# Half-made output tiles: starting an attention block's output projection on the heads that are already finished

## What is computed

```
o_fox = fox_attention(fq, fk, fv, log_f)                 # 8 heads of 64, a forget gate
o_nsa = nsa_attention(nq, compress(kc), compress(vc),     # 8 heads of 64; three branches:
                      ks, vs, kw, vw, gates)              #   compressed, selected, window
y = concatenate([o_fox, o_nsa], axis=-1) @ w_out          # [512,1024] @ [1024,1024]
x = x + rms_norm(y, g[1])
mem_n = rms_norm(mem, mem_norm_g)                         # 256 memory rows
x = x + rms_norm(memory_cross_attention(rms_norm(x, g[2]), mem_n, ...), g[3])
```

## Time and profile before

| | |
|---|---|
| time, median of 3 runs | 2358.0 (2357.14 to 2361.31) |
| profiled execution: its time | 2356.57 |
| profiled execution: its span | 2354.6 |
| PE busy | 2195.7 (93%) |
| DVE, ACT, POOL busy | 53%, 47%, 31% |
| granted TensorE clock, mean | 0.969 |

### The profile page before, as it was taken

The page is one execution under the profiler, slowest core; times in us unless marked ns, Lnnn a source line. Parts: engine busy times, 40 slices in busy tenths (PEclk is TensorE's granted clock), DMA queues, the critical chain, the costliest instruction groups (busy, mean ns, idle before and its releaser), DMA issues.

```text
span 2354.6 us, 29885 instructions
## 1 busy us (share of the span) xinstructions
PE 2195.7 (93%) x10776; PEld 1776.7 (75%) x10776; DVE 1239.3 (53%) x2212; ACT 1118.4 (47%) x1964; POOL 726.9 (31%) x479
## 2 busy tenths in 40 slices
PE   8989999989999999988979999999988888999997
PEld 6656677767888787766867888887867767888886
DVE  6776575558999634555455232224467455332223
ACT  6455554467888535545343332224666344322222
POOL 4361233410000221511234333225833424333233
PEclk9999999999999999998989999999999989999999
DMA  4402233218999530220212232331311221332331
GB/s 165 151 24 68 72 104 107 72 72 306 394 387 394 190 102 25 72 81 1 90 63 67 96 100 96 99 99 63 99 54 37 72 72 48 98 105 91 99 99 54
DMA packets 74529, 264.10 MB, mean 112 GB/s; under 512 B 8272, under 2 KB 8400, under 8 KB 74000
## 3 DMA queue, kind: packets, MB, share of 16 engines
q1 hardware_dynamic: 66816, 238.76, 29.3%
q0 software_dynamic: 2816, 11.82, 1.4%
q10 hardware_dynamic: 4752, 11.61, 1.3%
HBM read 247.98 MB, written 14.18 MB: 111 GB/s over the span
## 4 chain that ended last, share of the span: by engine, by line
PE 80%; DVE 7%; ACT 6%; issue 3%; POOL 2%; DMA 2%; POOLq 0%; DVEq 0%; SPq 0%; ACTq 0%
PE ps L512 17%; PE ps L514 17%; PE ps L513 17%; PE ps L1144 3%; PE ps L574 2%; PE ps L1159 2%; PE ps L2855 2%; PE ps L2857 2%; PE ps L2856 2%; PE ps L1178 2%; PE ps L550 2%; PE ps L551 2%; PE ps L556 2%; PE ps L2882 1%; PE ps L2883 1%
## 5 line engine op out<-in xcount | busy, mean ns | idle before, releaser
L454 ACT ACTIVATE wh<-raw 128x1024 fp32r<-128x1024 f32 x308 | 322.3, 1054 | 443.4 <-PE ps L514 413.2
L459 DVE TENSOR_TENSOR wl<-raw,wh 128x1024 fp32r<-128x1024 f32 x176 | 238.8, 1363 | 512.7 <-ACT wh L454 507.5
L459 POOL TENSOR_TENSOR wl<-raw,wh 128x1024 fp32r<-128x1024 f32 x132 | 318.2, 2411 | 489.1 <-ACT wh L454 473.2
L512 PE MATMUL ps<-hh,wh 128*128 128x512 f32 (+1 forms) x1192 | 468.0, 393 | 0.3 <-DVE wl L459 0.3
L514 PE MATMUL ps<-hh,wl 128*128 128x512 f32 (+1 forms) x1192 | 464.5, 390 | 0.0
L513 PE MATMUL ps<-hl,wh 128*128 128x512 f32 (+1 forms) x1192 | 464.4, 390 | 0.0
L512 PE MATMUL ps<-act,wh 128*128 128x512 f32 (+1 forms) x688 | 270.5, 393 | 13.8 <-ACT act L1419 9.9
L513 PE MATMUL ps<-act,wh 128*128 128x512 f32 (+1 forms) x688 | 268.5, 390 | 0.0
L514 PE MATMUL ps<-act,wl 128*128 128x512 f32 (+1 forms) x688 | 268.3, 390 | 0.0
L512 PEld LDWEIGHTS ps<-hh,wh 128*128 128x128 f32 (+1 forms) x1192 | 223.7, 188 | 48.9 <-issue 2.1
L514 PEld LDWEIGHTS ps<-hh,wl 128*128 128x128 f32 (+1 forms) x1192 | 223.5, 188 | 47.6 <-issue 0.6
(11 more groups left out here) (468 smaller groups left out, 3887.1 us busy)
## 6 DMA issues: line engine op xcount, KB each, us to landing
raw<-d_w SPq DMA_DIRECT2D x277, 512.0 KB, 3.7
raw_x<-d_moe SPq DMA_DIRECT2D x84, 512.0 KB, 6.4
raw<-d_moe SPq DMA_DIRECT2D x84, 512.0 KB, 6.6
d_xs<-Sb POOLq DMA_DIRECT2D x7, 514.0 KB, 8.8
Xb<-d_xs ACTq DMA_DIRECT2D x6, 514.0 KB, 6.0
area<-d_mem POOLq DMA_DIRECT2D x3, 1024.0 KB, 6.5
d_ys<-rows ACTq DMA_DIRECT2D x6, 512.0 KB, 6.3
xT<-d_x SPq DMA_DIRECT2D x8, 256.0 KB, 6.7
```

What stands on the lines that cost most here:

```text
L454: me.e.activation(hi, raw, ACT.Copy).then_inc(*me.done("wh", m))
L459: me.e.tensor_tensor(lo, raw, hi.bitcast(F32), ALU.subtract).then_inc(*me.done("wl", m))
L512: me.e.matmul(bank[0:m, 0:n], wh[:, c], hi, start=k == 0, stop=False)
```

## The change

The attention functions of ACT and DVE get a hook `last`, called in their closing step. There, and in POOL's program behind its attention, `fox_out` now splits the four "of" chunks, with a narrower wait list. PE, after its last attention step, begins the output tiles n = 0, 1, 2 on chunks 0 to 3 only (`begun_pe`, 12 matmuls each), one before and two behind what is left of the compressed branch; `sandwich_pe` later adds chunks 4 to 7 to them. The blocks of the weights change order accordingly: tile A (the first) holds the first halves of n = 0 and n = 1, tile B the first half of n = 2 and the second of n = 0, tile C the second halves of n = 1 and n = 2; D is n = 3, E is n = 4, as before.

```diff
-def linear(K, me, key, name, layer, columns, src, m=128, n=T, row0=0, after=None, pool="ps", amid=None):
-    bank = K.banks[me.take(pool, *key)]
-    for k, (hi, lo, ready) in enumerate(src):
+def linear(K, me, key, name, layer, columns, src, m=128, n=T, row0=0, after=None, pool="ps", amid=None, ks=None):
+    k0, k1 = ks or (0, len(src))
+    bank = K.bank(*key) if k0 else K.banks[me.take(pool, *key)]
+    for k in range(k0, k1):
+        hi, lo, ready = src[k]
...
-    if after is not None:
+    if after is not None and k1 == len(src):
         me.give(pool, key, *after)
...
+        if last and step > len(pairs):
+            last(K, me)
         if step > 1:
             scales_act(K, me, a, p - 1, pairs[p - 1][0])
...
+def begun_pe(K, me, v, name, n, src, k1):
+
+    linear(K, me, ("sw", v, n), name, 0, cols(128 * n, 128 * n + 128), src, ks=(0, k1))
+    K.plan.tile["begun", v, n] = (len(K.plan.blocks) - 1) // 8 if K.plan.dry else K.plan.tile["begun", v, n]
...
-        linear(K, me, ("sw", v, n), name, layer, cols(128 * n, 128 * n + 128), src, after=[("y", v, n)])
+        linear(K, me, ("sw", v, n), name, layer, cols(128 * n, 128 * n + 128), src, after=[("y", v, n)],
+               ks=(begun[1] if n < begun[0] else 0, len(src)))
...
     attention_pe(K, me, "nsa", K.i_branch, ticks=2)
     me.alias("hfree", "n4")
+    outs = K.parts(0, 4, 4, "of") + K.parts(8, 12, 4, "on")
+    for n in range(3):
+        begun_pe(K, me, "x4", "ev_w_out_2", n, outs, 4)
+        me.tick(2)
     me.flush()
     me.alias("end", "pe", "nsa")
-    sandwich_pe(K, me, "x4", "ev_w_out_2", 0, K.parts(0, 4, 4, "of") + K.parts(8, 12, 4, "on"), "mem1")
+    sandwich_pe(K, me, "x4", "ev_w_out_2", 0, outs, "mem1", (3, 4))
...
+def fox_out(K, me):
+
+    ahead(K, me, ("begun", "x4", 0))
+    war = [("S", "nsa", 7, h, g) for h in range(2) for g in range(3) if h == 0 or g != 1] + [("S", "nsa", 7, 1, 1)]
+    war += [("cmp", "s", half) for half in range(2)] + [("xin", s, half) for s in range(2) for half in range(2)]
+    parts_of(K, me, "of", 4, 0, lambda c: K.area[:, 20 + c, :], [("whole", "of", c) for c in range(4)], war)
...
 def even_out(K, me):
     war = [("end", "pe", "nsa"), ("end", "dve", "nsa")]
-    parts_of(K, me, "of", 4, 0, lambda c: K.area[:, 20 + c, :], [("whole", "of", c) for c in range(4)], war)
     parts_of(K, me, "on", 4, 8, lambda c: K.O[:, c, :], [("cmp", "add", c) for c in range(4)], war)
...
     attention_pool(K, me, "nsa", K.i_branch, ticks=2)
+    fox_out(K, me)
     me.flush()
```

More of the change, by code:

```diff
@@ L1319, in attention_pe, with attention_act @@
     me.alias("end", "pe", a)
-def attention_act(K, me, a, items, first=(), pt_first=(), ticks=0):
+def attention_act(K, me, a, items, first=(), pt_first=(), ticks=0, last=None):
     pairs = pairs_of(items)
@@ L1336, in attention_act, with attention_dve @@
     me.alias("end", "act", a)
-def attention_dve(K, me, a, items, first=(), pt_first=(), ticks=0):
+def attention_dve(K, me, a, items, first=(), pt_first=(), ticks=0, last=None):
     pairs = pairs_of(items)
@@ L2220, in residual_pool, with sandwich_pe @@
         values_pool(K, me, ("mv", side), K.mem_values(side))
-def sandwich_pe(K, me, v, name, layer, src, side=None):
+def begun_pe(K, me, v, name, n, src, k1):
+    linear(K, me, ("sw", v, n), name, 0, cols(128 * n, 128 * n + 128), src, ks=(0, k1))
+    K.plan.tile["begun", v, n] = (len(K.plan.blocks) - 1) // 8 if K.plan.dry else K.plan.tile["begun", v, n]
+def sandwich_pe(K, me, v, name, layer, src, side=None, begun=(0, 0)):
     for n in range(DC):
@@ L3574, in even_act @@
     me.beside = compressed_side(K, me)
-    attention_act(K, me, "nsa", K.i_branch, [("end", "pe", "fox")], [("pv", "fox", 3)], ticks=2)
+    attention_act(K, me, "nsa", K.i_branch, [("end", "pe", "fox")], [("pv", "fox", 3)], ticks=2, last=fox_out)
     me.flush()
@@ L3599, in even_dve @@
     K.o_last = [("out", "nsa", c) for c in range(4)]
-    attention_dve(K, me, "nsa", K.i_branch, [("end", "pe", "fox")], [("pv", "fox", 3)], ticks=2)
+    attention_dve(K, me, "nsa", K.i_branch, [("end", "pe", "fox")], [("pv", "fox", 3)], ticks=2, last=fox_out)
     me.flush()
```

## The result

| | before | after |
|---|---|---|
| time, median of 20 runs each | 2357.21 (2351.22 to 2362.66) | 2363.07 (2355.29 to 2373.28) |
| ratio, with 95% interval | | 1.0024 [1.0014, 1.0034] |
| profiled execution: time, span | 2356.57, 2354.6 | 2360.35, 2358.5 |
| granted clock, mean | 0.969 | 0.966 |

A forecast was written before the change was run, and what follows sets the result against it. The memory's chain sets the start of n = 3, with PE only 1.08 behind; spreading 2.9 later plus 2.0 for the clock makes +4.9, and 2358.0 + 4.9 = 2362.9, range 2357.8 to 2367.0.

The forecast's parts named there:

- Begun halves on PE: At the end of attention, PE starts the begun halves at 1109.0, with a gap of some 1.5 instead of 3.64.
- "On" halves 3.0 later: ACT's "on" halves wait for tile A's end on PE and start at 1115.6 instead of 1112.58.
- Load 2.0 later: The memory load, queued behind POOL's "on" low halves, is issued at 1120.1 instead of 1118.11.
- The load's landing, 7.2: The memory load lands 7.2 after issue, 0.7 of it for a weight load issued within 1 of it.
- The Trainium skill's round robin: DMA engines alternate between queues, so the weight load costs the memory load 2.0 instead of 0.7; sum 1.3 higher.
- Landing to root, 8.4: From the memory's landing to PE's spreading takes 8.4, against 8.1, with POOL's low half of E beside DVE's sums.
- The 6.2: Lower end for landing to PE's spreading, if POOL and DVE don't meet.
- Spread 2.9 later: PE's spreading matmuls ahead of n = 3 come at 1135.7 instead of 1132.77.
- 7 to 8 was forecast: Sign in the profile after: PE waits 7 to 8 for the memory's sums, ahead of line 574's four matmuls.
- Clock, 2.0: After PE's wait, n = 3 begins at half clock and loses 2.0, from a span of 1.4 to 2.7.
- Rival 3: The clock also drops in PE's begun halves, delaying the "on" halves and load: +2.7, 2365.6; chance 0.10.
- Rival 4: PE's lead counts: with the root by 1127, n = 3 begins 6.0 sooner, giving 2352.0; chance 0.04.

The follow-up runs named there:

- e1: Changed kernel with the end of attention marked earlier on PE, so the "on" halves no longer wait for tile A; 2360.12, ratio to before 1.0024.
- e2: Changed kernel with the memory load put into half of the score buffer and issued ahead of the "on" halves; 2354.24, ratio to before 0.9986.
- e4: Changed kernel with 26 idle matmuls on PE in its wait ahead of the memory's column sums; 2359.56, ratio to before 1.0014.
- e8: Changed kernel itself, unaltered, run again for a second profile; 2363.43, ratio to before 1.0035.
- e5: Changed kernel with ACT's split of tile E moved behind all eight of the memory's squares; 2362.98, ratio to before 1.0021.
- e10: Changed kernel with only six idle matmuls added on PE in the gap ahead of the begun halves; 2361.43, ratio to before 1.0022.
- e6: Changed kernel with only output tile n = 0 begun early, instead of n = 0 to 2; 2358.46, ratio to before 1.0007.
- e7: Changed kernel with both the "on" halves freed from tile A and the memory load issued early; 2353.89, ratio to before 0.9988.
- e9: Changed kernel with "on" halves freed, memory load early and six idle matmuls in PE's gap ahead of the begun halves; 2353.2, ratio to before 0.9978.

## Why the prediction was right, and where its steps were off

The forecast, 2362.9 and slower as likely as not, met the measured 2363.07, and the mechanism is the one predicted: the "on" halves wait for tile A, the memory load behind them goes out later, PE's hole is filled at one place and opens at another, and the clock falls in it. e1 undoes the first link, e2 the load's dependence and e4 the fall of the clock. The seams follow in all three; of the times only e2's does, those of e1 and e4 can't be told from the changed kernel's. The first profile's 3.34 are 1.44 at the spread and 1.90 behind it. e1 takes away the first part and keeps a clock loss, e4 does the reverse; both together weren't run.

The hit is closer than the steps deserve, and part of it is luck. The forecast of a difference was 4.9 and the measured one is 5.9; it came within 0.2 of the time only because it was added to the median of 3 runs, 2358.0, where 20 runs gave 2357.21. And the 4.9 itself has two errors that nearly cancel: the landing was priced too high, and the fall of the clock at the begun halves was left to a rival of 0.10.

Step by step, as differences of offsets from T0:

- *Begun halves on PE.* Predicted: start at 1109.0 with a gap of 1.5. Measured: 1109.38 with a gap of 1.44, where T0 itself is 0.41 later. Right.
- *"On" halves 3.0 later.* Measured 10.38 - 6.98 = 3.4. The cause, tile A's end, is right: the row names PE. Load 2.0 later: measured 2.1.
- *The load's landing, 7.2.* This is the step that failed. With a weight load issued 1.2 behind it, it took 5.27 in the first profile (1.3 less than before, where 0.7 more was put in), 6.1 in e8, and 5.73, 6.2, 5.95 and 5.42 in e1, e4, e5 and e10. With none beside it, it took 6.55 before and 5.68 in e6. So no delay by the weight load shows; what makes single landings differ by 1.3 stays open. The Trainium skill's round robin (DMA: Bandwidth & Descriptors, "Queues, rings and completion order") would have given 7.2 + 1.3 = 8.5; no run here shows such a share lost.
- *Landing to root, 8.4.* Measured 8.71, +0.6 on before where +0.3 was put in. The four sums took 4.04 beside POOL's low half, as the earlier trace rows said, and e5 confirms the cause. The 6.2 that the prediction gave for POOL and DVE apart is more than its own terms make (8.1 - 1.23 - 1.0 = 5.9); e5 measured 6.73.
- *Spread 2.9 later.* Measured 1.44 in the first profile: 2.12 (load) - 1.28 (landing) + 0.60 (landing to root). The landing makes the whole shortfall. PE's wait ahead of the sums is shorter with it, 5.50 and in e8 6.39, where 7 to 8 was forecast.
- *Clock, 2.0.* Measured 1.90 from the spread to the end of the seam, and e4 shows it by itself. (Another 0.5, in the column sums, was in the term before.) Profiles with a wait of 3.86 to 6.39 ahead of the sums lose 1.6 to 2.8; those with none or up to 0.50 lose nothing (27.46 to 27.49). Here the term is over half of the first profile's 3.34. The Trainium skill (TensorE: Matmul & The Clock Gate, "Part 1: The HAM clock gate") calls this penalty under 1% of a typical kernel, which agrees (1.9 of 2360 is 0.08%), and advises against fitting a count of slow matmuls; for a change worth 0.2% that advice leaves out too much.
- *Rival 3, the clock falling in the begun halves*, had 0.10. It is true of one of the changed kernel's two profiles and adds 2.2 to the seam there, 1.6 of it by the slow half. Its price was too high (+2.7) and, as five of eight profiles with such a gap show the fall, its chance too low: the earlier trace rows showed idle time spread thinly over a stretch, not one gap behind thin matmuls. This puts back what the landing left out.
- *Rival 4*, a faster kernel, needed a load that doesn't stand behind the "on" halves. e2, e7 and e9 are that kernel; the forecast for it was 6.0 less than before at n = 3, and e9 has 4.2.

The first profile's seam (+3.3) and the second's (+5.6) both lie in the interval of the measured difference, 3.3 to 8.0. How often each course is taken in the timed runs stays open.

## What to carry to other kernels

Work moved ahead into an engine's hole gains only if that engine is the one waited for next; look for what the moved work now stands in front of, above all a completion signal that covers more than its name says (here the end of the attention, which became the end of a weight tile). First free the longest chain that ends at the seam (here a load queued behind vector work), and then fill the hole: the same begun halves cost 3 to 6 in one order and gained in the other. Price a pause of TensorE at what it loses after it too. Where a pause can't be avoided, idle matmuls in it can hold the clock; in e4, e9 and e10 they cost nothing on the path.

## What was not expected of the hardware

- The same gap of 1.44 behind the same 8 matmuls was followed by a granted clock of 1.00 in the profiles of after, e1 and e4, and by a lower one (0.72 or 0.73 over a window of 6) in those of e2, e5, e6, e7 and e8; it cost 1.5 to 1.6 each time. In e5, e7 and e8 the first two matmuls behind the gap still ran at full clock (0.31 and 0.23 from start to start, then 0.43). What differs between these executions, no row shows.
- The memory load (1 MB) landed no later with a 512 KB weight load issued 1.2 behind it: 5.3 to 6.2 in six profiles, against 6.55 (before) and 5.68 (e6) with none.
- Moving PE's pause doesn't only shift the slow stretch: waits of 3.9 (e1, e5) lost 2.7 to 2.8, waits of 5.5 to 6.4 lost 1.6 to 2.3. The longer waits had slowed the column sums already (1.19 to 1.20 against 0.68), which adds 0.5 to theirs; even so the longer wait was not clearly the dearer one.
